# A hybrid trunk step on one core: low weights in pieces of 512 columns, and norm scale columns made a stage earlier

## The reference

```
def rms_norm(x, g):
    y = x32 * lax.rsqrt(jnp.mean(x32 * x32, axis=-1, keepdims=True) + NORM_EPS)
    return y.astype(x.dtype) * g
def adaln(cond, w, b):
    m = jax.nn.silu(cond) @ w + b          # shift, scale, gate for mixer and for FFN
    return jnp.split(m, 6, axis=-1)
def swiglu(h, w1, w3, w2):
    return (jax.nn.silu(h @ w1) * (h @ w3)) @ w2
# layer 0, mixer: HGRN2 (gated linear recurrence) and mLSTM (matrix memory), 4 heads each
#   p = h @ w_in_even (1024 x 4624); o = recurrences(p); mix @ w_out_even (1024 x 1024)
# layer 1, mixer: windowed attention with sinks (8 q heads, 2 kv heads) and latent attention (8 heads)
#   p = h @ w_in_odd (1024 x 1440); softmax(q k) v; mix @ w_out_odd (1024 x 1024)
# per layer: h = rms_norm(x, g) * (1 + scale) + shift;  x = x + gate * f(h)
```

## Time and profile before

| | |
|---|---|
| median of three runs | 1258.39 us |
| the profiled execution, its own time | 1258.74 us |
| its span, first to last instruction | 1256.8 us |
| TensorE busy | 1156.2 us, 92% |
| VectorE busy | 482.6 us, 38% |
| ScalarE busy | 430.6 us, 34% |
| GpSimd busy, all but 0.4 us in line 1012 | 479.3 us, 38% |
| mean granted TensorE clock | 0.952 of full speed |
| chain that ended last: TensorE, VectorE, ScalarE, GpSimd | 70%, 17%, 3%, 2% |

### The profile page before, as it was taken

The page is one execution under the profiler, slowest core; times in us unless marked ns, Lnnn a source line. Parts: engine busy times, 40 slices in busy tenths (PEclk is TensorE's granted clock), DMA queues, the critical chain, the costliest instruction groups (busy, mean ns, idle before and its releaser), DMA issues.

```text
span 1256.8 us, 17140 instructions
## 1 busy us (share of the span) xinstructions
PE 1156.2 (92%) x7238; PEld 1050.6 (84%) x7238; DVE 482.6 (38%) x822; ACT 430.6 (34%) x658; POOL 479.3 (38%) x119
## 2 busy tenths in 40 slices
PE   5699987999979999999999979777998999999997
PEld 3499987987758899999999869565587999999996
DVE  4524999415669411111111140427658111101112
ACT  0442421362243432232222242445625333333222
POOL 0244454420005245445445523112022555554652
PEclk9599999998999899999999989887998999999998
DMA  9743332254423676665566653042016344443441
GB/s 312 248 126 103 101 101 68 68 184 134 135 84 101 169 209 192 178 192 157 159 197 193 166 172 67 17 118 67 1 35 167 101 134 123 114 122 112 119 116 51
DMA packets 242939, 163.83 MB, mean 130 GB/s; under 512 B 20215, under 2 KB 241454, under 8 KB 242863
## 3 DMA queue, kind: packets, MB, share of 16 engines
q1 hardware_dynamic: 214880, 135.74, 37.4%
q10 hardware_dynamic: 27982, 26.99, 6.8%
HBM read 159.81 MB, written 2.90 MB: 129 GB/s over the span
## 4 chain that ended last, share of the span: by engine, by line
PE 70%; DVE 17%; ACT 3%; DMA 3%; issue 3%; POOL 2%; ACTq 1%; SPq 0%; DVEq 0%
PE banks L410 17%; PE banks L411 17%; PE banks L412 17%; PE banks L484 3%; DVE sq L1479 3%; POOL w_lo L1012 2%; DVE h_lo L1455 1%; DVE ht L1465 1%; DVE Qd L1630 1%; DMA raw<-in_ada_w 1%; PE banks L908 1%; DMA raw<-in_w_in_even 1%; PE banks L450 1%; PE banks L452 1%; PE banks L451 1%
## 5 line engine op out<-in xcount | busy, mean ns | idle before, releaser
L1012 POOL TENSOR_TENSOR w_lo<-raw,w_hi 128x2048 fp32r<-128x2048 f32 (+4 forms) x115 | 479.1, 4167 | 754.7 <-ACT w_hi L1035 754.7
L410 PE MATMUL banks<-h_hi,w_hi 128*128 128x384 f32 x1152 | 393.2, 341 | 24.2 <-DVE h_lo L1455 18.6
L411 PE MATMUL banks<-h_lo,w_hi 128*128 128x384 f32 x1152 | 388.0, 337 | 0.0
L412 PE MATMUL banks<-h_hi,w_lo 128*128 128x384 f32 x1152 | 387.8, 337 | 0.0
L1035 ACT ACTIVATE w_hi<-raw 128x2048 fp32r<-128x2048 f32 (+4 forms) x115 | 193.5, 1683 | 205.5 <-PE banks L412 157.4
L410 PEld LDWEIGHTS banks<-h_hi,w_hi 128*128 128x128 f32 x1152 | 217.9, 189 | 35.5 <-issue 29.5
L411 PEld LDWEIGHTS banks<-h_lo,w_hi 128*128 128x128 f32 x1152 | 218.2, 189 | 0.7
L412 PEld LDWEIGHTS banks<-h_hi,w_lo 128*128 128x128 f32 x1152 | 217.8, 189 | 0.6
L1508 DVE TENSOR_TENSOR uf<-sa,banks 128x384 f32<-128x384 f32 x44 | 24.4, 554 | 328.3 <-PE banks L412 322.4
L410 PE MATMUL banks<-u_hi,w_hi 128*128 128x384 f32 x352 | 118.6, 337 | 0.4 <-POOL w_lo L1012 0.3
L412 PE MATMUL banks<-u_hi,w_lo 128*128 128x384 f32 x352 | 117.7, 334 | 0.0
(11 more groups left out here) (348 smaller groups left out, 1326.3 us busy)
## 6 DMA issues: line engine op xcount, KB each, us to landing
raw<-in_ffn_w SPq DMA_DIRECT2D x88, 512.0 KB, 5.1
raw<-in_ada_w SPq DMA_DIRECT2D x28, 1024.0 KB, 5.5
raw<-in_ffn_w SPq DMA_DIRECT2D x32, 704.0 KB, 4.6
vada_raw<-in_ada_w ACTq DMA_DIRECT2D x20, 1024.0 KB, 6.2
raw<-in_w_in_even SPq DMA_DIRECT2D x18, 1024.0 KB, 5.3
raw<-in_w_out_even SPq DMA_DIRECT2D x4, 1024.0 KB, 6.2
raw<-in_w_in_odd SPq DMA_DIRECT2D x3, 1024.0 KB, 7.1
raw<-in_w_in_odd SPq DMA_DIRECT2D x8, 256.0 KB, 4.6
```

The lines of the kernel that those rows point to most:

```text
L410: pe.matmul(out, s_hi, m_hi, start=first and j == 0, stop=False)
L411: pe.matmul(out, s_hi, m_lo, start=False, stop=False)
L412: mm = pe.matmul(out, s_lo, m_hi, start=False, stop=last and j == len(terms) - 1)
L1012: pool.tensor_tensor(w_lo[s % SPLIT][:, 0:n], raw[u % RAW][:, 0:n], w_hi[s % SPLIT][:, 0:n].bitcast(F32), ALU.subtract).then_inc(S["lo_rea ...
```

## The change

Two edits. GpSimd's one subtraction per unit becomes a loop of subtractions over 512 columns at most: 2048 columns are 4 instructions, 1408, 1280 and 1152 are 3, 512 and 128 stay 1. The semaphore `lo_ready` is raised by the last. And `gains(n)` is taken out of `norm(n)`: for n = 0 it stands directly ahead of the norm as it did, for n = 1 behind the modulation of the mLSTM norm, for n = 2 ahead of the residuals of the down projection of layer 0, for n = 3 ahead of the rotary part of layer 1.

```
-                pool.tensor_tensor(w_lo[s % SPLIT][:, 0:n], raw[u % RAW][:, 0:n],
-                                   w_hi[s % SPLIT][:, 0:n].bitcast(F32), ALU.subtract).then_inc(S["lo_ready"], 1)
+                for at in range(0, n, 512):
+                    to = min(at + 512, n)
+                    ins = pool.tensor_tensor(w_lo[s % SPLIT][:, at:to], raw[u % RAW][:, at:to],
+                                             w_hi[s % SPLIT][:, at:to].bitcast(F32), ALU.subtract)
+                ins.then_inc(S["lo_ready"], 1)
...
-                gains(n)
                 dve.wait_ge(S["rstd_ready"], n + 1)
...
                 low_u(FT - 1)
+                if l == 0:
+                    gains(2)
...
             biases_to(4)
+            gains(0)
             norm(0, 0, "norm0")
...
             modulation("mlstm_norm")
+            gains(1)
...
+            gains(3)
             dve.wait_ge(S["odd_in"], 16)
```

## The result

The changed kernel took 1252.3 us in the median of four runs (1250.8 to 1255.4), beside 1258.95 us for the kernel before in the same session (1258.4 to 1259.7): a ratio of 0.9943, 95% interval 0.9915 to 0.9971. The forecast was 1252.0 and a chance of 0.62 for faster. The profiled execution of the changed kernel took 1250.8 us (span 1248.9), 8.0 us less than that of before.

What follows compares the result with a forecast made beforehand. TensorE, busy 92% of the span, was taken as the bound, with only its waits for VectorE to win. Terms -7.0 - 3.2 + 0.6 + 2.0 + 0.8 + 0.3 = -6.5 on 1258.7 gave 1252.2, median 1252; range 1243 to 1263.5.

Steps and rivals of the forecast that it cites:

- HGRN2, -7: HGRN2 levels: TensorE's waits for Kd shrink, -9.1 us, against a value unit starting about 2 us later; -7 in all.
- the third rival: HGRN2 levels: pieces meet Qd, Qd, Kd, Kd as well, costing 4.0 us instead of 4.27; total 1259 us; chance 0.22.
- Attention, -3.2: Attention: two pr instructions take 2.8 us instead of 4.91, less 0.5 given back, twice: -3.2 us.
- Gains, +0.6: Norms 1 and 3: ht is freed earlier but meets the block's fourth piece, 0.3 us later at each: +0.6 us.
- Serial places, +2.0: Where TensorE waits for a low part, or norm 2's modulation weights, longer blocks add 0.38 or 0.26 us each: +2.0 us.
- the up projection of layer 1, +0.8: Up projection of layer 1: slack 0.30 against +0.38, so every second unit stalls 0.08 us: +0.8 us.
- Norm 0, +0.3: Norm 0: VectorE, held up 3.7 us once, is now held up by four pieces of 1.0 us: +0.3 us.
- the third unit's 0.38: Third unit at 73.7, where TensorE waits for a low part: the longer block adds 0.38 us.
- longer blocks: GpSimd's blocks of 2048 columns take 0.38 us more: +2.0 us where TensorE waits, +0.8 in layer 1's up projection.
- The ports don't stay with GpSimd: Rival that GpSimd's next piece keeps the shared ports, each hold-up lasting 0.38 us longer: 1266 us; chance 0.12.
- the waits did not all go: Rival that late pieces fit VectorE's pauses: HGRN2 -13, attention -5, the rest +3, so 1243.5 us; chance 0.12.
- The second rival: GpSimd's blocks: a piece costs 0.35 us more, savings shrink to 7; total 1268 us; chance 0.08.

Runs made afterwards that it cites:

- the extra pause: The changed kernel with one more wait of VectorE for its own instruction at the levels, between SF and PX: 1253.45 us (before 1259.2), ratio 0.9959.
- the split alone: The changed kernel with the gains back inside the norms, blocks still in pieces of 512 columns: 1253.3 us (before 1257.9), ratio 0.9959.
- ten blocks: The changed kernel with pieces of 512 only in six input blocks of layer 0, two query and two output blocks of layer 1: 1244.5 us, ratio 0.9898.
- the complement: The changed kernel with six input blocks of layer 0, two query and two output blocks of layer 1 whole, pieces elsewhere: 1266.1 us, ratio 1.0073.
- 1024 and 256: The changed kernel with pieces of 1024 in blocks 11 to 16, 256 in blocks 73 and 74, whole blocks elsewhere: 1243.9 us, ratio 0.9873.
- the levels free: Whole blocks, gains moved, only the first 128 columns' low part in the last six input blocks of layer 0: 1242.7 us (before 1259.2), ratio 0.9865.
- 512 and 256: The changed kernel with pieces of 512 in blocks 11 to 16, 256 in blocks 73 and 74, whole blocks elsewhere: 1241.7 us, ratio 0.9855.

## Why the prediction was right, and where it was not

The sum was -6.5 and the profiled executions differ by 8.0, the medians by 6.65. The mechanism is the one predicted: a piece ends VectorE's wait earlier, and TensorE stops waiting for VectorE. Two things in it came out by luck, the order of the pieces in the levels and the way that two wrong terms cancel. (One reading is off by little: the excess at 189.87 ends 0.12 us before GpSimd's subtraction does, not 0.15.) Its terms were these:

- **HGRN2, -7.** Right, and the step on which the rest hung: from VectorE's wait for one piece, twice a level, to the level's period. It came to -7.5 from the third unit to L719, of which 0.9 is the clock behind the last wait, left out of the sum. PF 1.93 us, level 11.8 and last `Kd` 3.1 were as forecast, and the value unit waited 2.40 us instead of 0.20, 2.2 more (2 predicted). Which pieces VectorE waits for was not as forecast (3 and 4, not 1 and 2), and at one level, from 165.95 on, the third rival's picture is there: the pieces met the queue Qd, Kd, Kd, SF and cost 4.4 us. Whole blocks at the value unit and pieces in the levels gave 9.1, the number that the prediction had ahead of that subtraction.
- **Attention, -3.2.** The size was off: -5.5. The `pr` pair was right (2.68 for 2.8), and two pairs give 2 x 2.23 = 4.5 us. The 1.0 us that I gave back for pieces 3 and 4 hitting the small statistics was too much: they do hit them (the rows at 849.76 and 858.60 wait 1.0 us each), but by the end of TensorE's second long wait for `pr` only 0.2 us of the first 1.0 is lost (it comes 22.92 us into the stage before and 18.66 after), since VectorE's pauses behind it, in which it waits for TensorE and ScalarE, became shorter. Before, TensorE came out of both long waits (2.88 and 4.02 us) at half clock, 1.2 GHz: six products of L908 took 1.54 us, and the granted clock was 0.55 from 856.1 to 859.9 and 0.50 from 867.0 to 872.8. After, with a wait of 2.38 us, they took 0.87 at 2.4 GHz (the row at 857.48), but the clock fell right behind them: the next twelve products took 1.55 us, as in the kernel before. So the slow stretches became fewer and did not go. Behind the second wait, where before has its 5.8 us at half clock, the stage gains the last 1.2 us. I put them down to the clock, which I had left out of the sum.

```profile
867.06 1.54 PE L908 MATMUL banks<-const,pr 128*128 128x128 f32 x6 [4.02 <-DVE pr L1834]
```

and after, behind the row at 857.48:

```profile
858.28 1.55 PE L924 MATMUL banks<-pT,vt 128*64 128x128 f32 x12
```

- **Gains, +0.6.** The mechanism was right, the size half: the first `ht` pair of norm 1 started 0.1 us behind `rstd`, but took 1.64 us instead of 0.75 beside the fourth piece and ended 0.15 us later relative to the block (0.3 predicted). With the gains in the norm it is the same.
- **Serial places, +2.0, and the up projection of layer 1, +0.8.** Undersized: the stages without a busy VectorE lost 5.3 us. The first up units lost 0.42 and 0.41, as predicted, and the second down units 0.28 and 0.25. But after norm 2, where I had one term of 0.38, both the modulation weights and the next input unit came later, 1.0 us in all. And in the up projection of layer 1 GpSimd's blocks come alternately 8.49 and 8.35 us apart instead of 8.32, which is +0.10 a unit, 1.8 us over the projection; I had 0.04.
- **Norm 0, +0.3, and the third unit's 0.38.** Not to be told from the scatter of the start. With pieces of 512 the first `h_lo` came at 55.0 to 55.8 us in four traces and with whole blocks at 57.0 to 59.4 in seven, but by the third unit this is gone: it starts at 78.2 to 79.0 and at 77.8 to 80.3.

Attention and longer blocks were off by 2.3 and 2.5 us, with opposite signs, which is why the total fits better than its terms. That is luck.

*The rivals.* The ports don't stay with GpSimd: PF takes 1.93 us, where this rival wanted 5.6 or more. A cut costs 0.14 us and not 0.35. Turn by turn without profit happened at one level only. And the waits did not all go: 3.1 us ahead of the last level stayed.

*The port rule.* The prediction set the Trainium skill's page "SBUF — State Buffer", section "SBUF: two separate sides", by which whoever starts first has the ports for its whole instruction, against the earlier trace rows. By these rows and those of the runs, exclusion for the whole instruction is borne out: VectorE waited 1.0 us beside 512 columns and 2.2 beside 1024 (and 0.4 to 0.5 beside 256, where PF took 1.38 and SI 1.48). That the first to ask comes first is not: the piece that started at 191.80 waited 5.4 us through six products of VectorE that started after it, and with the extra pause it went in there.

*TensorE's clock* makes much of the scatter between executions. The stage from L719 to L695 has the same work in all kernels: 80.4 us in the profiles before and after, 83.6 with the split alone, 86.9 with pieces in ten blocks, 77.2 in the complement. With 1024 and 256 it is 86.9 as well, with the levels free 85.4, and with 512 and 256 it is 80.4. The stretches read 0.94, 0.86 and 0.98 in the clock column (second last but two) for before, the ten blocks and the complement:

```profile
281.00:361.00 80.00, 75.07 (x506) 54.66 (x504) 51.13 (x77) 23.16 (x67) 0.00 (x0) 0.94 0.39 125
```

```profile
271.00:357.00 86.00, 81.45 (x506) 58.91 (x504) 50.84 (x77) 22.70 (x66) 0.00 (x0) 0.86 0.36 115
```

```profile
286.00:362.00 76.00, 71.53 (x505) 52.66 (x503) 50.58 (x76) 22.36 (x66) 0.00 (x0) 0.98 0.41 130
```

So the profile of the ten blocks is 6.4 us longer there at a lower clock, in work that the change doesn't touch, and the median of six, 1244.5, is the better number than the profiled 1250.0. That it is chance is likely and not shown: with 512 and 256, which has the same pieces in the levels, the stage took 80.4, but the other three kernels with whole blocks behind shorter levels took over 85.

What stays open is whether the attention's last 1.2 us are the clock. In the four kernels with pieces of 512 there the stage took 68.87 to 68.91 us at granted clocks of 0.88 to 0.93, so a slow stretch costs nothing where TensorE waits for VectorE anyway; with 256 it took 66.2 to 66.8 us, at 0.94 to 0.96. The kernel before had 0.87 and 74.37. No run separated the clock from the waits.

## What to carry to other kernels

Where two engines exclude each other, cut the long instruction only where the short ones lie on the path: the same cut won 13 us in ten blocks and lost 8 in the rest. Price both sides from rows, the cost of a cut (0.14 us here) and the wait of one piece, and look in which stage the low side has no slack: 0.3 us of slack was used up by 0.42. And when a stage gets shorter, everything that is paced by it comes at another point of it, so a count of who meets whom holds for one piece size only.

## What the runs showed of the hardware

- A slow stretch of TensorE costs what the granted clock says where TensorE itself is the limit: behind the last `Kd` wait the stage took 61.22, 60.35, 60.09 and 58.74 us at 0.74, 0.83, 0.86 and 1.00 over its first ten us. In the attention, where it waits for VectorE, 0.88 and 0.93 over the stage gave the same 68.9.
- VectorE keeps the ports through a queue of instructions without a pause. A piece of GpSimd's took 6.65 us behind six products of 0.87, and got in where VectorE waited for its own semaphore, a pause of 0.1 us.
- Once VectorE has had to wait for the ports itself, they alternate, one piece and one instruction, pause or not. At 166 us, with GpSimd's next piece always ready, four products in a row took 2.04 instead of 0.94 us, 4.4 us for one level. In the kernel with the extra pause four products do the same from 157.36 on. These two places are the evidence; no run tests the rule by itself. The rows of the changed kernel:

```profile
165.95 1.10 DVE L1635 TENSOR_TENSOR Qd<-q,PF 128x768 f32<-128x768 f32 x1
166.97 2.04 DVE L1635 TENSOR_TENSOR Qd<-q,SI 128x768 f32<-128x768 f32 x1
168.93 2.04 DVE L1635 TENSOR_TENSOR Kd<-kf,SF 128x768 f32<-128x768 f32 x1
170.90 2.05 DVE L1635 TENSOR_TENSOR Kd<-kb,PX 128x768 f32<-128x768 f32 x1
172.87 2.05 DVE L1635 TENSOR_TENSOR SF<-SF,PF 128x768 f32<-128x768 f32 x1
174.84 0.95 DVE L1635 TENSOR_TENSOR PX<-PX,SI 128x768 f32<-128x768 f32 x1
```

- A subtraction on GpSimd costs 0.14 us for each cut back to back: 4.62, 5.04 and 5.59 us for 2048 columns in one, four and eight instructions. The second rival's 0.35 us did not appear. The prediction took the Trainium skill's page "GPSIMD Engine Reference", section "Instruction dispatch", as speaking for it; that section tells of a dispatcher on each of eight cores but puts its call at tens of cycles only, so it names no cost of 0.35 us, and here all that an instruction costs of its own, this included, is no more than 0.14 when they follow each other.
